# The cosine half of a rotary embedding moved from GpSimd to VectorE in a two-model fp32 kernel

## What is computed

```python
def apply_rope(x):
    ...
    return jnp.concatenate([x1 * c - x2 * sn, x1 * sn + x2 * c], axis=-1).astype(x.dtype)

def dsa_attention(xn, w_in, w_o):
    q, k, v, qi, ki, wi = jnp.split(xn @ w_in, A_SPLITS, axis=-1)
    q = apply_rope(q.reshape(b, s, A_HEADS, HEAD_DIM))
    k = apply_rope(k.reshape(b, s, A_KV_HEADS, HEAD_DIM))
    qi = apply_rope(qi.reshape(b, s, IDX_HEADS, IDX_DIM))
    ki = apply_rope(ki[:, :, None, :])[:, :, 0]
    ...
    idx_logits = jnp.einsum('bqhd,bsd->bqhs', qib, ki)
    score = jnp.einsum('bqhs,bqh->bqs', jax.nn.relu(idx_logits), wib)
    _, sel = lax.top_k(score, n_sel)
```

## Time and profile before

| | us |
|---|---|
| runs shown | 1551.24, 1553.61, 1556.23 |
| their median | 1553.61 |
| the profiled execution: time | 1553.99 |
| the profiled execution: span | 1552.2 |

### The profile page before, as it was taken

One profiled execution on the slowest core, in us unless ns is written; L12 is line 12 of the kernel. 1 busy time (PEld: TensorE's weight loads), 2 busy tenths in 40 slices (PEclk: granted clock), 3 DMA queues, 4 the chain that ended last, 5 costly groups with the idle time before them and its releaser, 6 DMA issues.

```text
span 1552.2 us, 28644 instructions
## 1 busy us (share of the span) xinstructions
PE 1462.2 (94%) x12411; PEld 1274.0 (82%) x12411; DVE 863.3 (56%) x1360; ACT 708.0 (46%) x1212; POOL 120.8 (8%) x114
## 2 busy tenths in 40 slices
PE   3999999998999999789999896999999999999997
PEld 1997887886797899589999795679999799689996
DVE  2457644447476444665555558445555648665555
ACT  2433533344465323454444444445444557554443
POOL 0000000011001534300000010000000014000000
PEclk8999999999998999899999897599999999989999
DMA  9999799744243000045565243025556454355551
GB/s 357 384 324 305 252 352 309 258 158 156 82 138 119 19 4 3 1 167 190 190 190 176 87 139 104 0 82 189 185 175 188 129 169 137 109 176 191 190 189 56
DMA packets 177429, 257.17 MB, mean 166 GB/s; under 512 B 10424, under 2 KB 122360, under 8 KB 177304
## 3 DMA queue, kind: packets, MB, share of 16 engines
q1 hardware_dynamic: 177304, 255.35, 49.8%
HBM read 254.28 MB, written 1.05 MB: 164 GB/s over the span
## 4 chain that ended last, share of the span: by engine, by line
PE 85%; DVE 8%; ACT 3%; issue 2%; DMA 1%; SPq 1%; POOL 0%; DVEq 0%; ACTq 0%; POOLq 0%
PE un L1772 14%; PE un L1773 13%; PE un L1774 13%; PE acc L1813 9%; PE acc L1814 9%; PE acc L1815 9%; PE acc L2045 4%; PE misc L1897 3%; DVE w_lo L1225 2%; DMA ada_buf<-in_ada_w 1%; PE acc L2171 1%; PE misc L2045 1%; PE un L2045 1%; ACT junk_later L781 1%; PE acc L1823 1%
## 5 line engine op out<-in xcount | busy, mean ns | idle before, releaser
L1225 DVE TENSOR_TENSOR w_lo<-stage,w_hi 128x1024 fp32r<-128x1024 f32 (+1 forms) x378 | 452.3, 1235 | 330.9 <-ACT w_hi L750 330.7
L750 ACT ACTIVATE w_hi<-stage 128x1024 fp32r<-128x1024 f32 (+1 forms) x378 | 379.0, 1048 | 245.1 <-PE acc L1815 223.8
L1772 PE MATMUL un<-h_hi,w_hi 128*128 128x256 f32 x1536 | 449.4, 293 | 0.2 <-DVE z_lo L1272 0.2
L1773 PE MATMUL un<-h_lo,w_hi 128*128 128x256 f32 x1536 | 440.0, 286 | 0.0
L1774 PE MATMUL un<-h_hi,w_lo 128*128 128x256 f32 x1536 | 439.4, 286 | 0.0
L1772 PEld LDWEIGHTS un<-h_hi,w_hi 128*128 128x128 f32 x1536 | 300.1, 195 | 15.2 <-issue 9.3
L1773 PEld LDWEIGHTS un<-h_lo,w_hi 128*128 128x128 f32 x1536 | 300.1, 195 | 1.1 <-issue 0.7
L1774 PEld LDWEIGHTS un<-h_hi,w_lo 128*128 128x128 f32 x1536 | 299.9, 195 | 0.0
L1813 PE MATMUL acc<-w_hi,z_hi 128*128 128x512 f32 x640 | 252.3, 394 | 0.0
L1814 PE MATMUL acc<-w_lo,z_hi 128*128 128x512 f32 x640 | 249.7, 390 | 0.0
L1815 PE MATMUL acc<-w_hi,z_lo 128*128 128x512 f32 x640 | 249.4, 390 | 0.0
(11 more groups left out here) (318 smaller groups left out, 1765.4 us busy)
## 6 DMA issues: line engine op xcount, KB each, us to landing
stage<-in_mlp_w SPq DMA_DIRECT2D x64, 1024.0 KB
ada_buf<-in_ada_w SPq DMA_DIRECT2D x48, 1024.0 KB, 7.9
stage<-in_w_up SPq DMA_DIRECT2D x32, 1024.0 KB
stage<-in_w_down SPq DMA_DIRECT2D x32, 1024.0 KB
stage<-in_conv_w_in SPq DMA_DIRECT2D x12, 1024.0 KB
stage<-in_rw_w_rkv SPq DMA_DIRECT2D x12, 1024.0 KB
stage<-in_w_in_a SPq DMA_DIRECT2D x8, 1024.0 KB
stage<-in_w_kv_b SPq DMA_DIRECT2D x8, 1024.0 KB
```

The costliest lines, as they stand in the source:

```text
L750: A_(w_hi[u % 2][:, half, 0:n], stage[u % NSTAGE][:, half, 0:n], ACT.Copy).then_inc(hi_made, 1)
L1225: V.tensor_tensor(w_lo[u % 2][:, half, 0:n], stage[u % NSTAGE][:, half, 0:n], w_hi[u % 2][:, half, 0:n].bitcast(F32), ALU.subtract).then_i ...
L1772: MM(out, hi_l, hi_r, start=start, stop=False, skip_group_check=True)
L1773: MM(out, hi_l, lo_r, start=False, stop=False, skip_group_check=True)
```

## The change

GpSimd's loop over the eight cosine products goes, with its waits and the semaphore `cos_done`. VectorE makes each product itself, as the first instruction after its wait for TensorE's rotated halves, ahead of the sine product; the sum no longer waits for GpSimd. Buffers, sizes and all other lists stay.

```diff
-        ROPE_USE = (0, 1, 2, 3, 5, 6, 7, 8)
         ROPE_KI, ROPE_QI, ROPE_K, ROPE_Q, N_ROPE = 0, 1, 3, 4, 8
...
-        rot_done, rope_done, ki_loaded, cos_done, kdup_ready = (sem(n) for n in ("rot_done", "rope_done", "ki_loaded", "cos_done", "kdup_ready"))
+        rot_done, rope_done, ki_loaded, kdup_ready = (sem(n) for n in ("rot_done", "rope_done", "ki_loaded", "kdup_ready"))
...
-            pool.wait_ge(const_b_in, 16)
-            for r in range(N_ROPE):
-                n = 1 if r == ROPE_KI else 2
-                if r == ROPE_KI:
-                    pool.wait_ge(sem("ki_loaded"), 1)
-                else:
-                    pool.wait_ge(un_free, freed(V_A + ROPE_USE[r]))
-                if r:
-                    pool.wait_ge(sem("rope_done"), r)
-                G.tensor_tensor(rope_c[:, 0:n, :], rope_in[r % 2][:, 0:n, :], c_("cos").unsqueeze(1).to_broadcast([P, n, SEQ]), ALU.mult)\
-                    .then_inc(sem("cos_done"), 1)
...
             def rope(r, n, dst):
                 dve.wait_ge(rot_done, r + 1)
+                V.tensor_tensor(rope_c[:, 0:n, :], rope_in[r % 2][:, 0:n, :], bc4(c_("cos"), n), ALU.mult)
                 link(V.tensor_tensor(dst, misc[:, 0:n, :], bc4(c_("sin"), n), ALU.mult))
-                dve.wait_ge(cos_done, r + 1)
                 V.tensor_tensor(dst, dst, rope_c[:, 0:n, :], ALU.add).then_inc(rope_done, 1)
```

## The result

| | before | after |
|---|---|---|
| median of 20 runs each, us | 1555.11 (1550.47 to 1559.71) | 1559.89 (1554.70 to 1562.78) |
| ratio, 95% interval | | 1.0026 (1.0014 to 1.0038) |
| the profiled execution, us | 1553.99 | 1562.05 |
| its span, us | 1552.2 | 1560.3 |

The ratio is about 4.0 us of 1555, with an interval from 2.2 to 5.9. The prediction was +2.9 us or 1.0019, called "the same" by the bound of 0.3%; it lies inside the interval.

A forecast was written before the change was run, and what follows sets the result against it. VectorE was taken to bound the projections up to the first logits, TensorE the attention behind. Five products, 3.05 us, less 0.13 for the port gave +2.92 on the 1553.61 median: 1556.5 us, range 1551.5 to 1560.5.

The forecast's parts named there:

- Which products count: Attention projections: K's and four query products lie on VectorE's path; the first three cost nothing, at most 1.8 us.
- The price: VectorE's added products: 0.61 us each, at most 0.72; five on the path make 3.05 us.
- The removed wait: VectorE's sums no longer wait for GpSimd's product: gain 0, at most 0.2 us.
- The port: Shared memory port: VectorE's first split behind the K rotation no longer slowed by GpSimd's product, -0.13 us.
- The sum by the letter: Skill page's exclusion rule taken literally: 0.26 us given back to GpSimd's end, making the sum +2.8 us.
- TensorE's waits: Projections: waits for VectorE's sums grow, the first from 0.33 to about 1.5 us, but slack covers them.
- B: Attention: the higher clock comes earlier, making the kernel faster, 1546.5 us; chance 0.06.
- C: Projections: the clock falls, slowing the last query unit; 1557.0 to 1561.6 us, middle 1559.3; chance 0.14.
- D: Added products don't show: fewer than five count or the loss is given back; 1553.6 to 1555 us; chance 0.14.
- The size: Whole kernel: 1556.5 us, +0.19%, against the 1553.61 median of the runs shown; called the same, chance 0.78.

The follow-up runs named there:

- e6: Kernel before with only the first three cosine products (index key, index queries) made by VectorE; split ahead of the K rotation to first logits 41.26 us, 0 over before.
- e7: Kernel before with only the K cosine product made by VectorE; split ahead of the K rotation to first logits 41.88 us, 0.61 over before.
- e4: Kernel before with only the four query cosine products made by VectorE; split ahead of the K rotation to first logits 43.57 us, 2.30 over before.
- e5: Kernel after with each cosine product made twice, the second waiting for the first; split ahead of the K rotation to first logits 47.79 us.
- e3: Kernel after without the eight cosine products, the sum taking the rotary input; split ahead of the K rotation to first logits 41.15 us, ratio 1.0001.
- e9: Kernel before with GpSimd's product for the first queries made twice in a row; split ahead of the K rotation to first logits 42.37 us.
- e8: Kernel after with K's and the first query product moved into VectorE's idle times; split ahead of the K rotation to first logits 42.97 us.
- e11: Kernel after with two output-projection weight splits moved into the attention's loop; split ahead of the K rotation to first logits 40.00 us.
- e12: Kernel before, two output-projection splits moved into the attention's loop, one score-choice round moved ahead of the third query rotation; ratio 0.9957.
- e2: Kernel after, unchanged, profiled once more; split ahead of the K rotation to first logits 44.17 us, ratio 1.0026.

## Why the prediction was right, point by point

**Which products count.** Right in every part, and shown one set at a time. The first three cost nothing (e6), K's costs its full step although VectorE idles for 3.98 us behind it (e7, 0.61), and the four query products cost theirs (e4). That the idle time was no cover is the point of the argument that could most easily have gone the other way. It was decided by following the wait past the engine that it names: from ScalarE's split back to the score activation that VectorE's own sums had released.

**The price.** 0.61 us per product and not its duration of 0.69: measured 2.30 + 0.13 over four, which is 0.61, and e5 shows the 0.72 for the product with a wait behind it. The five together were 3.05 less the port in the sum and 2.89 net in the stretch.

**The removed wait.** Worth nothing, as costed. In e7 and e4 some of these waits are in and some are out, and the steps are the same: 0.72 us from the sine product to the sum with GpSimd's wait between them and without it (941.18 to 941.90 in the kernel after).

**The port.** The sum's -0.13 was right: 10.65 + 30.50 in e3, where nothing but the port differs, is 0.12 less than before. The sum by the letter of the Trainium skill's page ("SBUF — State Buffer", 0.26) was too large here. e9 gives a reading of this by which that rule still holds. The first half split started 0.27 us before GpSimd was done and lost 0.12 of it. The second ended 1.07 us after GpSimd was done, where it takes 1.22 alone. In both about 0.15 us of the split seems to run while it is held. That is worked out from these two alone.

**TensorE's waits.** The first grew to 1.37 where about 1.5 was forecast, and the third to 5.98. A small one that I had not named came up, 0.24 us at the rotation of r = 6. The one ahead of the transposes was to grow from 6.66 to 7.2 us and stayed at 6.67, since the score products ahead of it took 0.58 us longer. None reached VectorE.

**The rivals.** B, an earlier rise of the clock in the attention: the rise came 54.0 us after the first logits in the kernel before and 54.7 in the kernel after, later and not earlier. Here luck had a part: in e4, e8, e9, e11 and e12 the rise did come earlier, at 51.8 to 53.0 us, and they ended 2.2 to 3.6 us sooner behind the logits than the kernel before. What decides this was not known when B got its chance of 0.06, and is not known now. C, a fall inside the projections that slows the last query unit: the clock stood at 1.00 from 943 to 950, while this unit ran. (The 938 to 945 of the prediction is the place of the unit in the kernel before; this execution came to it later.) D, products that do not show: refuted by e3 against e2, where the products alone make 3.02 us in the stretch and a ratio of 1.0001 against 1.0026.

**The size.** 1556.5 was said, and 1559.89 was measured. Of this 3.4 us, 1.5 is the reference: the three runs that the prediction started from had a median of 1553.61, and all 20 have 1555.11. The other 1.9 is the part of the difference of the medians, 4.8, that the stretch does not hold. The prediction put the rest of the kernel at nothing; the two profiles of the kernel after have 0.55 us there, behind the logits, with a later rise of the clock, and the remainder is not placed. So the sum is confirmed to 0.03 us where it was made, and the total only within an interval that is wider than the sum. Runs of one kernel spread over 8 to 9 us, and the ratio's interval takes 1.0019 in. "The same" by 0.3% was right, but close: the ratio is clearly above 1.

## What to carry to other kernels

An engine that is busy 56% of the span can be the whole path for 31 us, and have its part in a loop of waits for 10 us ahead of that. Before work is moved onto it, list its instructions in that stage and mark where its idle time ends on another engine, and whether that engine was waiting for it in turn: such idle time covers nothing. Where two executions of one kernel differ by more than the change can cost, measure a stretch between two instructions that both kernels have (here it repeats to 0.01 us while two spans of one kernel differ by 5.9), and use the spread of the total only for the total. Then sum up the granted clock outside the stretch, before the difference is put down to the change or called chance. And once the full stretch is known, look for what does not need to be in it: two weight splits moved behind it and one round of the choice moved inside it gained more than the cosine products could cost.

## What the runs showed of the hardware

- GpSimd and VectorE took strict turns in e9: a GpSimd product of 1.30 us took 2.16 and a VectorE half split of 1.22 us took 2.31 when each found the other at work. A single overlap of 0.27 us cost only 0.12.
- The start-to-start step of two VectorE instructions was 0.61 us for a 0.69 us product with nothing waiting for it, and 0.72 with a wait behind it, at every dose.
- The time to the same instruction, with nearly the same work ahead of it, wandered over 8.8 us between executions, and the times of one kernel over 9 us between runs. Both go with TensorE's granted clock: two executions of one program had 65 and 79 us at half clock ahead of the stretch and reached it 5.94 us apart.
- A wait of TensorE of 4.2 us, for nothing that the profile shows, stood at one place in 7 of the 14 executions. I did not find its cause. At like time at half clock they arrived 0.8 to 4 us later than those without it.
